# First layer's latent attention: norms applied behind the up-projections, weights scaled by the latent gains, heads staged at other places

## The chip, the cores and the metric

The kernel runs on one core of one Trainium2 chip. The metric is the device time of one execution in microseconds (us), the median of several runs. Its engines work side by side and are tied by semaphores: TensorE (PE in the profile, its queue of weight loads PEld), VectorE (DVE), ScalarE (ACT), GpSimd (POOL) and SyncE (SP), which here issues DMAs.

## What is computed

A trunk of two layers over two sequences of 512 tokens, each with 16 learned tokens in front, model width 1024. The first layer's mixer is multi-head latent attention beside a short gated convolution; the change touches only the attention part. Cut to that:

```python
def rms_norm(x, g):
    y = x * rsqrt(mean(x * x, axis=-1) + 1e-6)
    return y * g

z = h @ w_in                                  # h: the normed tokens
c_q, c_kv, k_r, g_b, g_c, u = split(z)        # 384, 256, 64 and three times 512 columns
q  = (rms_norm(c_q,  q_a_g)  @ w_uq ).reshape(tokens, 4, 192)
kv = (rms_norm(c_kv, kv_a_g) @ w_ukv).reshape(tokens, 4, 256)
k_nope, v = kv[..., :128], kv[..., 128:]
k = concat([k_nope, k_r repeated over the heads])
q, k = rms_norm(q, q_g), rms_norm(k, k_g)
q[..., 128:], k[..., 128:] = rotate(...)      # position tables, cos and sin
attn = softmax(q @ k.T * 192 ** -0.5) @ v
```

Everything else (the convolution, the output projections, the second layer's grouped attention, both SwiGLU blocks) stays as it is.

## The kernel before, in words

**Products.** Every float32 product is made of three matmuls of rounded halves: an operand is split into a high part (a ScalarE copy to the rounded type) and a low part (value minus high part, on VectorE or GpSimd). `product` (lines 166 to 170) issues the three, so nearly all matmuls have the lines 168, 169 and 170. Weights come by DMA from SP's queue into three slots of `stage`, ScalarE rounds them (`round_piece`, line 802) and GpSimd makes the low part (`split_piece`, line 806).

**The stages around the change.** Tokens lie in 10 tiles of 128 rows (5 for each sequence). `gates_steps` makes the convolution's columns of the first projection; `latent_steps` makes the latents and the heads; `attention_phase` runs the attention. Each engine has its own instruction list, written by `sync`, `scalar`, `gpsimd`, `tensor` and `vector` of the steps; an engine works its list strictly in order, so a wait holds up all that stands behind it.

1. **Key latents.** TensorE's `latent(0..9)`: 24 matmuls for each tile into bank 6 or 7. ScalarE's `copy_latent` (lines 823 to 828) takes the sum of squares and copies the tile out.
2. **Key ups, beside the query latents.** For each tile TensorE does `turn(i)` (transposes of the normed latent, line 928), `latent(NT + i)` (24 matmuls) and `up(i)` (12 matmuls of 512 columns). VectorE's `latent_rsqrt` finds the latents' inverse norms for half of the tiles at a time, `norm_latent` (line 1009) multiplies a tile by its inverse norm and by the gain row into `tmp`, from which the transposes read; `round_t` (ScalarE, line 835) and `split_t` (VectorE, line 1033) make the two parts of the transposed tile. ScalarE's `copy_up` (lines 844, 848) takes four sums of squares and copies the heads out, VectorE's `copy_values` (line 1024) the values, GpSimd's `scale_heads` (line 892) multiplies the copied keys by the gain row.
3. **Query ups.** For each tile `turn`, then `up(NT + i)` (18 matmuls of 384 columns); `copy_up`, `scale_heads` over 768 columns, and VectorE's `rotate_queries` (lines 693 to 698), which waits for `scale_heads`. `heads_rsqrt` finds the heads' inverse norms from the sums, by a chain of small operations on VectorE (lines 186, 187, 191 to 193), each of which waits for the one before. For the queries of the first sequence it is cut in two parts. Rotations of the last two tiles, and the inverse norms of the second sequence's keys and queries, are done inside the attention loop (`vector_at`, turns 2, 3, 5 and 7).
4. **Start of the attention.** A head is "staged" by GpSimd (`stage_keys`, lines 1611 and 1613; `stage_queries`, 1635 and 1637): head times inverse norm, into `stage`. TensorE then turns it (`prepare`: five items, keys' two chunks, queries' two chunks and a tail; lines 1798, 1787, 1790), ScalarE rounds (line 1712, 1720) and VectorE splits (1885, 1893). `items_after` says after which query up the first head's items come (the first three behind up 8, two behind up 9), `keys_after` and `queries_after` where GpSimd stages them (behind 5 and 6). The second head's items come in the attention's turns 1, 1, 2, 2 and 3.
5. **Attention loop.** 40 turns (8 heads, 5 query tiles): `scores` (with lines 1816, 1817), minimum on VectorE (1908), exponential on ScalarE (1736), reciprocal (1915), normalising on GpSimd (1672, 1676), turned probabilities (1829, 1835), output products. The exponentials' three buffers lie over `tmp`, `gain_rows` and `rope`; `wait_exponentials` keeps them from being written too early.

Line 1656 clears the tails. The position table is loaded twice, once into `rope` and, behind the weights of the query ups, once into `stage`.

## Time and profile before

| what | value |
|---|---|
| three runs | 2436.57, 2439.05, 2437.43 us; median 2437.43 |
| the profiled execution's own time | 2441.74 us |
| its span | 2439.9 us |
| granted TensorE clock, mean over the span | 0.98 of full speed |
| TensorE busy | 2335.1 us, 96% of the span |

The span is what the profile shows from first to last instruction; 1.8 us of the execution's own time lie outside it. The stages named above stand at these places of the span: key latents to 205 us, key ups to 278 us, query ups to 328 us, attention from 333 us. A row of the timeline has the start, the duration, the engine and line, the instruction with what it writes and reads, and in brackets how long the engine had been idle and what ended the wait. The granted clock is a share of full speed: TensorE's clock has two levels, 2.4 GHz (1.00) and 1.2 GHz (0.50), and a window's number is the mean.

### The profile page before, as it was taken

How to read it: one execution, taken by the hardware profiler on the slowest of the kernel's cores; microseconds unless marked ns; L12 is line 12 of the kernel's file. 1: busy time of each engine (PE TensorE's matmuls, PEld its weight loads, DVE VectorE, ACT ScalarE, POOL GpSimd, SP SyncE). 2: the span in 40 equal slices, each digit the busy share in tenths (PEclk: the TensorE clock that was granted, in tenths of full speed). 3: DMA queues.
4: the chain of work that ended last, by engine and by line, in shares of the span. 5: the costliest groups of instructions: out<-in, count | busy, mean ns of one | idle time of the engine just before them, and what ended most of it. 6: DMA issues, size and time to landing. Idle time of an engine off the chain costs nothing. (4 is left out here: it accounts for less than half of the span.)

```text
span 2439.9 us, 37816 instructions
## 1 busy us (share of the span) xinstructions
PE 2335.1 (96%) x14683; PEld 2130.8 (87%) x14683; DVE 1289.7 (53%) x2093; ACT 906.7 (37%) x1927; POOL 1239.4 (51%) x999
## 2 busy tenths in 40 slices
PE   7999969899999999999998998989999999999998
PEld 7999858899899999999997887888878888888886
DVE  5222667627744444444448467863864444444444
ACT  5125535535422222222225346664532222222221
POOL 1342457644655555555542346764465555555551
PEclk9999979999999999999998999999999999999999
DMA  5131100332211111111112100013211111111111
GB/s 205 44 122 43 42 1 1 135 102 84 61 48 53 48 48 48 43 51 48 53 40 74 39 2 1 2 44 95 82 52 52 52 52 53 52 53 52 53 52 74
DMA packets 186631, 137.69 MB, mean 56 GB/s; under 512 B 7260, under 2 KB 176360, under 8 KB 186456
## 3 DMA queue, kind: packets, MB, share of 16 engines
q1 hardware_dynamic: 186336, 135.20, 17.9%
q8 instruction: 119, 1.95, 0.3%
q14 instruction: 56, 0.46, 0.1%
q10 hardware_dynamic: 120, 0.09, 0.0%
HBM read 122.12 MB, written 12.85 MB: 55 GB/s over the span
## 5 line engine op out<-in xcount | busy, mean ns | idle before, releaser
L2251 POOL TENSOR_TENSOR w_lo<-stage,w_hi 128x512 fp32r<-128x512 f32 x384 | 517.2, 1351 | 638.5 <-ACT w_hi L2152 636.3
L2152 ACT ACTIVATE w_hi<-stage 128x512 fp32r<-128x512 f32 x384 | 239.3, 628 | 585.6 <-PE PS L170 583.0
L2460 DVE TENSOR_TENSOR hT<-hT,PS 128x528 f32<-128x528 f32 (+1 forms) x384 | 267.2, 696 | 335.1 <-PE PS L170 333.8
L168 PE MATMUL PS<-x_hi,w_lo 128*128 128x264 f32 (+2 forms) x1152 | 375.1, 326 | 13.2 <-POOL w_lo L2251 6.8
L169 PE MATMUL PS<-x_lo,w_hi 128*128 128x264 f32 (+2 forms) x1152 | 372.7, 323 | 0.0
L170 PE MATMUL PS<-x_hi,w_hi 128*128 128x264 f32 (+2 forms) x1152 | 372.6, 323 | 0.0
L168 PE MATMUL PS<-s_hi,w_lo 128*128 128x264 f32 (+1 forms) x1104 | 353.7, 320 | 3.1 <-DVE s_lo L2414 3.1
L170 PE MATMUL PS<-s_hi,w_hi 128*128 128x264 f32 (+1 forms) x1104 | 354.2, 321 | 0.0
L169 PE MATMUL PS<-s_lo,w_hi 128*128 128x264 f32 (+1 forms) x1104 | 353.1, 320 | 0.0
L168 PE MATMUL PS<-b_hi,w_lo 128*128 128x264 f32 (+1 forms) x864 | 279.6, 324 | 4.3 <-POOL w_lo L2251 4.3
L169 PE MATMUL PS<-b_lo,w_hi 128*128 128x264 f32 (+1 forms) x864 | 279.2, 323 | 0.0
L170 PE MATMUL PS<-b_hi,w_hi 128*128 128x264 f32 (+1 forms) x864 | 277.7, 321 | 0.0
L168 PEld LDWEIGHTS PS<-x_hi,w_lo 128*128 128x128 f32 x1152 | 219.7, 191 | 26.6 <-POOL w_lo L2251 7.2
L169 PEld LDWEIGHTS PS<-x_lo,w_hi 128*128 128x128 f32 x1152 | 219.3, 190 | 13.0
L170 PEld LDWEIGHTS PS<-x_hi,w_hi 128*128 128x128 f32 x1152 | 219.4, 190 | 12.8
L168 PEld LDWEIGHTS PS<-s_hi,w_lo 128*128 128x128 f32 x1104 | 207.7, 188 | 18.6 <-issue 3.7
L169 PEld LDWEIGHTS PS<-s_lo,w_hi 128*128 128x128 f32 x1104 | 207.4, 188 | 16.6
L170 PEld LDWEIGHTS PS<-s_hi,w_hi 128*128 128x128 f32 x1104 | 207.9, 188 | 15.8
L168 PEld LDWEIGHTS PS<-b_hi,w_lo 128*128 128x128 f32 x864 | 163.3, 189 | 21.0 <-POOL w_lo L2251 5.0
L170 PEld LDWEIGHTS PS<-b_hi,w_hi 128*128 128x128 f32 x864 | 163.5, 189 | 12.7
L169 PEld LDWEIGHTS PS<-b_lo,w_hi 128*128 128x128 f32 x864 | 162.9, 189 | 12.1
L168 PE MATMUL PS<-x_lo,w_lo 128*128 128x264 f32 (+1 forms) x480 | 154.5, 322 | 7.1 <-POOL w_lo L2251 7.1
(316 smaller groups left out, 4946.6 us busy)
## 6 DMA issues: line engine op xcount, KB each, us to landing
stage<-in_ffn_w SPq DMA_DIRECT2D x280, 256.0 KB, 2.8
stage<-in_even_w_out SPq DMA_DIRECT2D x32, 256.0 KB, 2.7
stage<-in_odd_w_out SPq DMA_DIRECT2D x32, 256.0 KB, 2.7
stage<-in_mla_w_in SPq DMA_DIRECT2D x12, 512.0 KB, 6.4
stage<-in_gqa_w_qkv SPq DMA_DIRECT2D x12, 512.0 KB, 3.8
h_spill<-hT SPq DMA_DIRECT2D x8, 528.0 KB, 5.1
hT<-h_spill SPq DMA_DIRECT2D x8, 528.0 KB, 6.8
conv_hi<-s_hi SPq DMA_DIRECT2D x4, 528.0 KB, 2.7
```

The costliest lines, as they stand in the source:

```text
L168: T.matmul(out, a_lo, b_hi, start=first, stop=False)
L169: T.matmul(out, a_hi, b_lo, start=False, stop=False)
L170: return T.matmul(out, a_hi, b_hi, start=False, stop=last)
L2152: A.activation(ring(w_hi, n), source(n), ACT.Copy).then_inc(rounded, 1)
L2251: G.tensor_tensor(ring(w_lo, n), source(n), ring(w_hi, n).bitcast(F32), ALU.subtract).then_inc(split, 1)
L2460: V.tensor_tensor(o, o, sums(st.slot), ALU.add).then_inc(drained, 1)
```

## The change

- The latents are no longer normed before they are turned: `turn` reads the copied latents as they are (it waits for `lat_copied`). The inverse norm is applied behind the up-projection, as ScalarE's scale in `copy_up` and as a scalar in `copy_values`. It is found for all ten tiles at once, and `latent_rsqrt(KV)` stands ahead of the first `split_t` on VectorE.
- The latent gains come in as five more columns of `gain_cols` (two more DMAs on ScalarE's queue; SP has two fewer). GpSimd's `scale_piece` multiplies the five pieces of up weights by them in `stage`, ahead of `round_piece`.
- The queries' gain goes into the keys' gain for the first 128 columns (`k_gain`), and into the position tables for the last 64 (`query_tables`, made by `make_tables` on GpSimd, in `rope`). `scale_heads` stays for the keys (`scale_keys`) and is gone for the queries. The second load of the position table is gone.
- The first head's keys are staged behind query up 0, its queries behind up 1 in the list (they wait for five rotations); items behind ups 2, 3, 7, 8, 8. The second head is staged ahead of the attention loop, its items come in turns 0, 0, 1, 2, 2.
- On VectorE the second sequence's key norms move to step `NT + 1`, the last two rotations to behind the last query up and into turn 1, the second sequence's query norms from turn 7 to 5. The first sequence's query norms are one piece.

```diff
-            g_rows = mid[0:44, 4224:4224 + P]
+            g_rows = mid[0:49, 4224:4224 + P]
...
-                for src, n in ((mla_q_a_g, Q_RANK), (mla_kv_a_g, KV_RANK), (mla_q_g, QK), (mla_k_g, QK)):
+                for src in (mla_q_g, mla_k_g):
...
+                for src, row, n in ((mla_q_a_g, 44, 3), (mla_kv_a_g, 47, 2)):
+                    act.dma_start(g_rows[row:row + n, :], src[0].rearrange("(c p) -> c p", p=P)).then_inc(gains_in, 16)
...
-                act.wait_ge(const_in, 16 * 5)
...
-                pe.wait_ge(gains_in, 16 * 5)
-                T.transpose(PS[:, 2, 0:44], g_rows, ident[0:44, 0:44]).then_inc(gains_t, 1)
+                pe.wait_ge(gains_in, 16 * 7)
+                T.transpose(PS[:, 2, 0:49], g_rows, ident[0:49, 0:49]).then_inc(gains_t, 1)
...
+            def scale_piece(pool, n):
+                kind, k = pieces[n]
+                column = 4 * KC + 3 * CONV_CHUNKS + (3 + k if kind == "ukv" else k)
+                raw = stage[:, (n % 3) * UNIT:(n % 3) * UNIT + widths[kind]]
+                pool.wait_ge(loaded[n % 3], 16 * ((gates.units + n) // 3 + 1))
+                G.tensor_tensor(raw, raw, gain_cols[:, column:column + 1].broadcast_to([P, widths[kind]]),
+                                ALU.mult).then_inc(w_scaled, 1)
+
             def round_piece(act, n):
-                act.wait_ge(loaded[n % 3], 16 * ((gates.units + n) // 3 + 1))
+                if n in scaled_pieces:
+                    act.wait_ge(w_scaled, scaled_pieces.index(n) + 1)
+                else:
+                    act.wait_ge(loaded[n % 3], 16 * ((gates.units + n) // 3 + 1))
...
-                sp.wait_ge(split, gates.units + number[("uq", 1)] + 1)
-                sp.dma_start(query_rope, line_rope).then_inc(table_in, 16)
...
                 def copy_up(n):
                     e, i = divmod(n, NT)
+                    r = rn_lat[e][:, i:i + 1]
+                    act.wait_ge(rn_ready, e + 1)
                     act.wait_ge(up_done, n + 1)
...
-                        last = A.activation(heads_to[e][:, i, hd * size:(hd + 1) * size], part, ACT.Square,
+                        last = A.activation(heads_to[e][:, i, hd * size:(hd + 1) * size], part, ACT.Square, scale=r,
...
+                def make_tables():
+                    pool.wait_ge(gates.const_in, 16 * 3)
+                    G.tensor_tensor(k_gain[:, 0:NOPE], k_gain[:, 0:NOPE], q_gain[:, 0:NOPE], ALU.mult).then_inc(tables_made, 1)
+                    shape = [P, TILES, 2, ROPE // 2]
+                    halves = q_gain[:, NOPE:QK].rearrange("p (w f) -> p w f", w=2).unsqueeze(1).broadcast_to(shape)
+                    for c in range(2):
+                        G.tensor_tensor(query_tables[:, :, :, c, :], tables[:, :, c, :].unsqueeze(2).broadcast_to(shape),
+                                        halves, ALU.mult).then_inc(tables_made, 1)
...
                 for n in range(4, 10):
+                    if n in scaled_pieces:
+                        scale_piece(pool, n)
                     split_piece(pool, n)
+                    if n == 4:
+                        make_tables()
+                pool.wait_ge(tables_made, 3)
                 for i in range(NT):
-                    scale_heads(i)
+                    if i in (4, 5, 7):
+                        scale_piece(pool, number[("uq", (4, 5, 7).index(i))])
+                    scale_keys(i)
                     if i in (4, 5, 7):
                         split_piece(pool, number[("uq", (4, 5, 7).index(i))])
+                pool.wait_ge(scaled, NT)
+                pool.wait_ge(lat_done, 2 * NT)
                 for i in range(NT):
-                    scale_heads(NT + i)
                     then(i)
...
                 def turn(n):
-                    pe.wait_ge(normed, n + 1)
+                    pe.wait_ge(lat_copied, n + 1)
...
-                        last = T.transpose(PS[:, t_bank(n), k * P:(k + 1) * P], tmp[:, at:at + P], ident[:, :])
+                        last = T.transpose(PS[:, t_bank(n), k * P:(k + 1) * P], lat[e][:, i, k * P:(k + 1) * P], ident[:, :])
...
             def rotate_queries(dve, link, i):
-                dve.wait_ge(scaled, NT + i + 1)
+                if i == 0:
+                    dve.wait_ge(tables_made, 3)
+                dve.wait_ge(up_copied, NT + i + 1)
...
-                    V.scalar_tensor_tensor(tmp[:, (n % 2) * Q_RANK:(n % 2) * Q_RANK + rank[e]], lat[e][:, i, 0:rank[e]],
-                                           rn_lat[e][:, i:i + 1], lat_gain[e], ALU.mult, ALU.mult).then_inc(normed, 1)
+                def latent_rsqrt(e):
+                    dve.wait_ge(lat_squared, (e + 1) * NT)
+                    link(V.tensor_scalar(v_stat[:, 0:NT], lat_ssq[e], 1.0 / rank[e], EPS, ALU.mult, ALU.add))
+                    rsqrt(link, v_stat[:, 0:NT], rn_lat[e], t_stat[:, 0:NT])
+                    V.engine_nop().then_inc(rn_ready, 1)
...
-                latent_rsqrt(KV, 0)
-                norm_latent(0)
+                latent_rsqrt(KV)
                 for n in range(2 * NT):
-                    if n + 1 < 2 * NT:
-                        norm_latent(n + 1)
                     split_t(n)
                     if n == NT:
-                        latent_rsqrt(Q, 1)
+                        latent_rsqrt(Q)
...
+                    if n == NT + 1:
+                        heads_rsqrt(dve, link, KV, 1)
...
                 then(NT - 1)
+                rotate_queries(dve, link, NT - 2)
...
-                if n in (2, 3):
-                    rotate_queries(dve, link, NT - 4 + n)
+                if n == 1:
+                    rotate_queries(dve, link, NT - 1)
                 if n == 5:
-                    heads_rsqrt(dve, link, KV, 1)
-                if n == 7:
                     heads_rsqrt(dve, link, Q, 1)
...
-            steps.items_after = {8: (0, 3), 9: (3, 5)}
-            steps.clear_after, steps.keys_after, steps.queries_after = 0, 5, 6
+            steps.items_after = {2: (0, 1), 3: (1, 2), 7: (2, 3), 8: (3, 5)}
+            steps.clear_after, steps.keys_after, steps.queries_after = 0, 0, 1
...
-                    elif u == 1 and L0:
-                        items_at.setdefault((1, 1, 2, 2, 3)[m], []).append(what)
...
                     if L0:
-                        stage_keys(1)
+                        stage_heads(1)
...
-                        if n == 0 and L0:
-                            stage_queries(1)
```

## Rows read from the trace of the kernel before

**Rows 1.** The page, part 1: busy time, share of span and instructions by engine.

```profile
PE 2335.1 (96%) x14683; PEld 2130.8 (87%) x14683; DVE 1289.7 (53%) x2093; ACT 906.7 (37%) x1927; POOL 1239.4 (51%) x999
```

**Rows 2.** Windows: length, busy time (and instructions) per engine, granted clock, DMA share, GB/s.

```profile
205.00:277.00 72.00, 72.00 (x385) 66.39 (x384) 29.36 (x81) 35.45 (x131) 21.00 (x14) 1.00 0.06 18
277.84:332.70 54.86, 42.35 (x227) 39.90 (x226) 36.36 (x88) 29.36 (x117) 26.26 (x18) 0.91 0.13 44
332.70:382.50 49.80, 34.96 (x206) 32.89 (x207) 35.95 (x85) 18.38 (x50) 28.66 (x31) 0.73 0.00 1
384.00:415.30 31.30, 29.63 (x245) 27.62 (x244) 23.19 (x54) 20.48 (x57) 24.66 (x30) 1.00 0.01 1
```

**Rows 3.** Windows of 4 us around one stop of TensorE.

```profile
308.00:312.00 4.00, 2.10 (x8) 2.10 (x9) 3.85 (x11) 0.49 (x1) 1.15 (x1) 0.65 0.01 2
312.00:316.00 4.00, 4.00 (x14) 4.00 (x13) 3.74 (x9) 0.00 (x0) 2.87 (x2) 0.50 0.00 0
316.00:320.00 4.00, 4.00 (x26) 3.93 (x26) 1.68 (x6) 2.63 (x11) 1.39 (x2) 1.00 0.00 0
```

**Rows 4.** Timeline of TensorE: start, duration, instruction, idle before and releaser.

```profile
209.74 0.39 PE L168 MATMUL PS<-up_first,t_kv 128*128 128x512 f32 x1
...
285.11 0.49 PE L928 MATMUL PS<-ident,tmp 128*128 128x128 f32 x3
...
288.62 0.49 PE L928 MATMUL PS<-ident,tmp 128*128 128x128 f32 x3
...
309.90 0.47 PE L928 MATMUL PS<-ident,tmp 128*128 128x128 f32 x1 [4.92 <-DVE tmp L1009]
...
332.70 0.34 PE L168 MATMUL PS<-x_hi,x_lo 128*106 128x264 f32 x1 [3.37 <-DVE x_hi L1893]
...
344.49 0.94 PE L1829 MATMUL PS<-ident,tmp 106*128 106x106 f32 x4 [5.53 <-issue]
...
366.24 1.12 PE L1798 MATMUL PS<-ident,stage 128*128 128x128 f32 x4 [4.76 <-DVE x_lo L1885]
```

**Rows 5.** Timeline of VectorE, 303 to 310 us.

```profile
303.29 1.70 DVE L187 TENSOR_SCALAR rn_all<-stat 128x20 int32<-128x20 int32 x1
...
307.47 1.73 DVE L193 SCALAR_TENSOR_TENSOR rn_all<-stat,rn_all 128x20 f32<-128x20 f32 x1
```

**Rows 6.** Timeline of GpSimd, 303 to 310 us.

```profile
303.12 1.83 POOL L892 TENSOR_TENSOR wide<-wide,gain_rows 128x768 f32<-128x768 f32 x1 [3.19 <-ACT wide L848]
304.91 1.27 POOL L1611 TENSOR_TENSOR stage<-hT,rn_all 128x640 f32<-128x640 f32 x1
...
307.35 1.81 POOL L892 TENSOR_TENSOR wide<-wide,gain_rows 128x768 f32<-128x768 f32 x1
```

**Rows 7.** Timeline of GpSimd, 197 to 209 us.

```profile
197.24 1.85 POOL L806 TENSOR_TENSOR s_lo<-stage,s_hi 128x768 fp32r<-128x768 f32 x1 [8.72 <-ACT s_hi L802]
...
206.53 2.41 POOL L806 TENSOR_TENSOR s_lo<-stage,s_hi 128x1024 fp32r<-128x1024 f32 x1
```

**Rows 8.** Timeline of ScalarE, 204 to 207 us.

```profile
204.56 1.04 ACT L802 ACTIVATE s_hi<-stage 128x1024 fp32r<-128x1024 f32 x1
...
206.45 0.53 ACT L828 ACTIVATE hT<-PS,stat 128x320 f32<-128x320 f32 x1
```

**Rows 9.** Timeline of VectorE, start of a chain of 12 small operations.

```profile
215.75 0.16 DVE L1001 TENSOR_SCALAR tmp<-stat 128x5 f32<-128x5 f32 x1
215.95 0.17 DVE L186 TENSOR_SCALAR stat<-tmp 128x5 int32<-128x5 int32 x1
```

**Rows 10.** Groups of instructions, ScalarE, 200 to 450 us, shapes apart.

```profile
L825 ACT ACTIVATE wide<-PS,stat 128x384 f32<-128x384 f32 x10 | 5.8, 582 | 21.7 <-PE PS L170 21.7
...
L835 ACT ACTIVATE x_hi<-PS 128x384 fp32r<-128x384 f32 x10 | 4.9, 488 | 3.6 <-PE PS L928 3.6
```

**Rows 11.** Timeline of ScalarE's queue and of TensorE, the first 9 us.

```profile
2.90 0.60 ACTq L387 DMA_DIRECT2D mid<-in_conv_w  x1
...
8.26 0.33 PE L557 MATMUL PS<-ident,mid 44*128 44x44 f32 x1 [0.93 <-DMA mid<-in_conv_w]
```

More of the change, by code:

```diff
@@ L181, in program, with rsqrt @@
         vec_steps = [0]
[L183 removed]
+        def rsqrt(link, v, y, t, negative=False):
             guess = float(0x5F3759DF - 2 ** 31 * negative)
@@ L676, in gates_steps @@
             steps.drained, steps.stored, steps.spilled, steps.y_split = drained, stored, spilled, y_split
+            steps.const_in, steps.gains_ready = const_in, gains_ready
             return steps
@@ L684, in program, with rope_heads @@
         v_stat, t_stat = tmp[:, 960:1024], stat[:, 68:68 + 64]
-        def rope_heads(dve, link, xs, cos, sin, scratch, heads, axes, half):
+        def rope_heads(dve, link, xs, tables, scratch, heads, axes, half):
             n = heads * axes * half
@@ L691, in rope_heads @@
             shape = [P, heads, axes, half]
-            c, s = cos.unsqueeze(1).broadcast_to(shape), sin.unsqueeze(1).broadcast_to(shape)
-            V.tensor_tensor(t[0], x1, c, ALU.mult)
-            V.tensor_tensor(t[1], x2, s, ALU.mult)
-            V.tensor_tensor(t[2], x2, c, ALU.mult)
-            link(V.tensor_tensor(t[3], x1, s, ALU.mult))
+            cos1, sin1, cos2, sin2 = (m.unsqueeze(1).broadcast_to(shape) for m in tables)
+            V.tensor_tensor(t[0], x1, cos1, ALU.mult)
+            V.tensor_tensor(t[1], x2, sin2, ALU.mult)
+            V.tensor_tensor(t[2], x2, cos2, ALU.mult)
+            link(V.tensor_tensor(t[3], x1, sin1, ALU.mult))
             V.tensor_tensor(x1, t[0], t[1], ALU.subtract)
@@ L711, in latent_steps @@
             loaded, rounded, split = gates.loaded, gates.rounded, gates.split
[L712 to L713 removed]
+            (lat_done, lat_early, lat_squared, lat_copied, rn_ready, turned, t_rounded, t_split, up_done,
+             up_squared, up_copied, v_copied, scaled, roped, keys_rotated, rn_k_ready, rn_q_ready, tables_made, w_scaled) = (
                 sem(f"lat_{x}") for x in (
[L715 to L716 removed]
+                    "done", "early", "squared", "copied", "rn_ready", "turned", "t_rounded", "t_split", "up_done",
+                    "up_squared", "up_copied", "v_copied", "scaled", "roped", "keys_rotated", "rn_k_ready", "rn_q_ready",
+                    "tables_made", "w_scaled"))
             KV, Q = 0, 1
@@ L784, in t_part @@
                 return (t_q if n >= NT else t_kv)[part][n % 2]
+            scaled_pieces = [n for n, (kind, k) in enumerate(pieces) if kind in ("ukv", "uq")]
             def load_piece(sp, n):
@@ L848, in copy_up @@
                     A.activation(heads_to[e][:, i, :].rearrange("p (b h n) -> p b h n", b=2, h=2),
-                                 src[:, :, :, 0, :] if e == KV else src, ACT.Copy).then_inc(up_copied, 1)
+                                 src[:, :, :, 0, :] if e == KV else src, ACT.Copy, scale=r).then_inc(up_copied, 1)
                 gates.scalar(act, round_piece)
@@ L1023, in copy_values @@
                     dve.wait_ge(up_copied, i + 1)
-                    V.tensor_copy(v_tok0[:, i, :].rearrange("p (b h n) -> p b h n", b=2, h=2),
-                                  ups(KV, 2 * (i % 2))[:, :, :, 1, :]).then_inc(v_copied, 1)
+                    V.tensor_scalar(v_tok0[:, i, :].rearrange("p (b h n) -> p b h n", b=2, h=2),
+                                    ups(KV, 2 * (i % 2))[:, :, :, 1, :], rn_lat[KV][:, i:i + 1], None,
+                                    ALU.mult).then_inc(v_copied, 1)
                 def split_t(n):
@@ L1086, in wait_exponentials @@
                 if n == 1:
-                    act.wait_ge(scaled, 2 * NT)
+                    act.wait_ge(keys_rotated, 1)
                 if n == 2:
-                    act.wait_ge(keys_rotated, 1)
+                    act.wait_ge(roped, NT)
             def wait_scores(pe, n):
@@ L1257, in rotate @@
                 table = tables[:, work[n][1] % TILES]
-                rope_heads(dve, link, xs, table[:, 0], table[:, 1], scratch, heads, 2, 32)
+                rope_heads(dve, link, xs, (table[:, 0], table[:, 1]) * 2, scratch, heads, 2, 32)
                 V.engine_nop().then_inc(roped, 1)
```

93 lines of the change are left out of this document (28 added, 65 removed).

## The prediction

> **What bounds the kernel now.** I read the page first: TensorE is busy 96% of the span [rows 1], so a gain must fill the places where it stands, or runs at its lower clock. The windows show where these are [rows 2]: none in the key ups (72.0 us busy of 72.0, clock 1.00); 12.5 us of standing in the 54.86 us from query up 0 to the first scores; 14.8 us in the 49.80 us of the attention's first ten turns, at a mean clock of 0.73. Ten settled turns take 31.30 us at 1.00. The timeline of TensorE names the stops [rows 4]: 4.92 us ahead of the turn for query up 5 (waiting for the normed latent), 3.37 us ahead of the first scores (waiting for the first head's tail), 5.53 and 4.76 us in the loop. What made the first is in VectorE's and GpSimd's rows side by side: a `heads_rsqrt` operation on 20 columns takes 1.70 or 1.73 us and ends when GpSimd's instruction ends (303.12 + 1.83 = 304.95 against 303.29 + 1.70 = 304.99; 307.35 + 1.81 = 309.16 against 307.47 + 1.73 = 309.20) [rows 5, 6]. Where GpSimd is quiet, such a chain steps on every 0.20 us [rows 9]. So a small operation that meets a GpSimd instruction waits for its end. After the stop the clock stays low: 0.65, 0.50, then 1.00 again [rows 3], so from 309.9 to about 316 us at half speed, 3.0 us lost.
>
> **The change, in order of the span.** The sum is made against the profiled execution, 2441.74 us (span 2439.9 and 1.84 around it), 4.3 above the median of 2437.43.
>
> (a) *Start.* Two more DMAs stand on ScalarE's queue, and TensorE's turn of the gains waits for all. That turn already waited 0.93 us for the last of them, issued at 2.90 in 0.60 us [rows 11]; VectorE's first scaling, and all after it, stands behind. Two more issues cost at most 1.2 us; nothing if they land with the others; a gain is excluded, since the turn waits for more. TensorE is the bound soon after, so it isn't recovered. I take **+0.7**. The two DMAs less on SP's queue and the dropped second table load (with its wait, nothing but values' loads behind it) stand beside full engines: 0.
>
> (b) *First key up.* Here the change adds a chain that TensorE sees. GpSimd finishes the low part of the last query piece but one at 199.1 [rows 7] and only then scales the first key piece. No row has this operation; 1024 columns cost 2.41 with two full operands [rows 7], and at the rate of a repeated operand 1024/640 x 1.27 = 2.0 [rows 6]. Nearest is the latter, I take 2.1: 201.2. ScalarE rounds, 1.04 [rows 8]: 202.3. Low part 2.4: 204.7; low part of the fourth query piece 1.85: 206.6; second key piece scaled: 208.7; rounded: 209.7. ScalarE's list has `copy_latent(9)` behind that rounding, so the tenth sum of squares, ready at 206.45 before [rows 8], comes 0.85 after: 210.6. All ten are now wanted before the first `split_t`. The first operation of `latent_rsqrt` meets GpSimd's low part (209.7 to 212.1) and waits for its end as in [rows 5, 6]; 12 operations of 0.20 then end at 214.5 [rows 9], `split_t` adds 0.4: up 0 starts at 214.9 and not at 209.74 [rows 4]. That is a stop of 5.2 us in a stage that had none, long enough by [rows 3, 4] to bring the clock down: 3.0 more. **+8.2**. Ends: 3.7 (the wait for GpSimd left out, 5.2 less 1.5, and the clock kept) to 10.5 (both scalings at 2.41, a slower return of the clock).
>
> The Trainium skill (GPSIMD Engine Reference, 3.1 Elementwise) gives 4497 ns for a `tensor_tensor` of 2048 float32 columns; half of that, 2.25, is an estimate for a scaled key piece, and by it (b) would be 0.3 larger. [Rows 6, 7] stand on either side of it, and no row shows this operation.
>
> The rest of the key ups: `norm_latent` off VectorE, scaled query pieces on GpSimd (busy 21.0 of 72 us), pointer scales on ScalarE (35.5 of 72): all under a full TensorE [rows 2], 0. `make_tables` (three operations under 1.3 us each, by the 640 columns of [rows 6]) falls in GpSimd's free time ahead of 197.24, before which it stood idle 8.72 us [rows 7]: 0.
>
> (c) *Query ups to first scores*, 54.86 us now. TensorE's own pace is 3.51 us for a tile (285.11 to 288.62) [rows 4], ten make 35.1. The first head's five items lie inside: four chunks of about 0.55 (1.12 at half clock [rows 4]) and a tail of 0.3, 2.5. Stalls that I expect: `heads_rsqrt(KV, 1)`, now at step 11, meets GpSimd's `stage_keys(0)`, which is free to start then: 1.1 on up 2. ScalarE's rounding of an item behind ups 2, 3 and 7: its work for a tile is near the pace, 0.3 each. The queries' norms (12 x 0.20) ahead of `split_t(17)`: 1.1. The last items ahead of `split_t(19)`: 0.6. `scale_heads`, which `rotate_queries` waited for, and `norm_latent`, whose lateness was the 4.92 us, are gone. Then the tail is split before up 9 ends, and the scores follow at once. 35.1 + 2.5 + 3.7 = 41.3: **-13.6**. Ends: 37.6 (no stall) to 47 (one of them long enough for the clock). The trace also prices the new scale: 384 columns take 582 ns with a pointer scale and 488 without [rows 10], so `copy_up`'s five activations grow by 0.47 us a tile. ScalarE, busy 29.36 us in this stage now, 2.9 a tile [rows 2], reaches 3.4: still under 3.51.
>
> (d) *First ten turns*, 49.80 us against 31.30 settled. Of the 18.5 us too much, 34.96 - 29.63 = 5.3 are TensorE at the low clock and 13.2 standing (14.84 less 1.67) [rows 2]; the stops of 5.53 and 4.76 us are the most of it [rows 4]. The first came with the second head's transposes, rotation of tile 8 and the first minimum all in turns 1 and 2; the second with the key norms of the second sequence, now gone to step 11. What is late next: VectorE has rotations 7 and 8 ahead of the first minimum, rotation 9 in turn 1, and 12 small operations in turn 5, between GpSimd's stagings. I leave 8.5 of the 18.5: 5.5 standing, 3 clock. **-10**. Ends: -15 to 0.
>
> Sum: 0.7 + 8.2 - 13.6 - 10 = -14.7; the profiled execution would take 2427.0, the median **2422.7**.
>
> **The rivals.**
> - *The gate is cheap*: GpSimd scales before ScalarE needs it, or the clock holds. Then (b) is about 2 and the median 2416.5. For it: VectorE idles there. Against: the lists' order leaves no freedom. 0.12.
> - *The start of the attention is jammed anew*. GpSimd's four staging operations for the second head (4 x 1.27 = 5.1 us [rows 6]) run while VectorE rotates tiles 7 and 8 ahead of the first minimum. By the rows' rule those small operations wait, the first minimum is up to 5 us later and the clock falls: 9 of the 10 of (d) are lost, 2431.7. 0.16.
> - *Sooner in name only*: the first head's queries still wait for five rotations and norms; (c) gives 9 instead of 13.6: 2427.3. 0.08.
> - *Slower*: the clock stays low after the stop at 210 us, through the key ups, where nothing hides it. At the 0.73 of the first turns [rows 2] 72 us become 98.6, 26.6 more in place of 3.0: 2446.3. It decides from a mean clock of about 0.80 down (72/0.80 = 90, 18 us, against the 17.7 gained otherwise). For it: the first ten turns. Against: these had a new stop every few us, while the key ups are full, and after the 4.92 us stop the clock came back in 6 us [rows 3]. 0.05.
>
> The Trainium skill (SBUF — State Buffer, Who interferes with whom) states the blocking of the second rival: an operation with two SBUF inputs and a GpSimd instruction that reads SBUF take the shared port in order of issue, and the second waits for the whole of the first. The trace agrees, by the four ends compared above. By that rule alone the loser may as well be GpSimd.
>
> **The numbers.** A measurement of this kernel tells about 0.2%, 4.9 us, from no change. My forecast has 0.59. Range 2412 to 2433: it takes in the cheap gate, the jam and the bounds of (b) and (c), not the slower case. Faster 0.84, the same 0.10 (the jam together with a dear gate), slower 0.06.
>
> **What would show it.** Right: a stop of about 5 us ahead of the first product of the key ups, near 210 us, then half clock for about 6; query ups at about 3.5 us a tile with no 4.92 us stop; first scores 41 us after query up 0; scores of turn 10 some 40 us after. Wrong: no stop near 210; a stop over 3 us between query up 9 and turn 3; a clock below 0.8 over the key ups.

## The result, and the profile after

| | kernel before | changed kernel |
|---|---|---|
| median | 2437.98 us (2436.57 to 2440.95, 7 runs) | 2431.02 us (2428.90 to 2431.75, 7 runs) |
| the profiled execution | 2441.74, span 2439.9 | 2430.68, span 2428.9 |
| ratio of the times | | 0.9969, 95% interval 0.9959 to 0.9979 |

The change takes 7.0 us off the kernel, 0.3%. The forecast was 2422.7 from 2437.43, a gain of 14.7: the time lies inside the range of 2412 to 2433, the gain is less than half of what was forecast.

The two profiles differ by more than the medians do: their spans by 11.0 us, their own times by 11.1. The profiled execution of before lies 3.8 us above the median of its runs, that of after 0.3 below. Two differences must be explained: 11.1 against the forecast's 14.7, and the 4.1 between 11.1 and 7.0.

The page's part 1, after; it answers to [rows 1]. TensorE is busy 5.1 us less, at the same number of instructions:

```profile
PE 2330.0 (96%) x14683; PEld 2124.9 (87%) x14683; DVE 1265.3 (52%) x2049; ACT 915.3 (38%) x1927; POOL 1229.5 (51%) x997
```

Windows of after, with the columns of [rows 2]: the key ups with the stop ahead of them, query up 0 to the first scores, first scores to the scores of turn 10, and ten settled turns.

```profile
205.00:284.00 79.00, 74.16 (x382) 67.54 (x380) 21.96 (x59) 39.80 (x131) 26.62 (x18) 0.96 0.05 16
284.84:332.94 48.10, 40.77 (x227) 39.22 (x226) 32.10 (x97) 31.51 (x108) 12.46 (x11) 0.93 0.14 50
332.94:372.07 39.13, 28.61 (x207) 26.67 (x206) 27.26 (x69) 20.69 (x59) 22.45 (x26) 0.87 0.00 1
374.00:405.30 31.30, 29.63 (x245) 27.62 (x244) 23.17 (x55) 20.45 (x57) 25.45 (x31) 1.00 0.01 2
```

The settled turns are what they were, 31.30 us. Query ups and start of the attention took 54.86 and 49.80 us [rows 2] and now take 48.10 and 39.13. But query up 0 starts at 284.84 where it started at 277.84. The timeline of TensorE names the stops, in brackets. The first is new. The next four, in the query ups, stand in the stage where [rows 4] had 4.92 us, and the last two, in the loop, where it had 5.53 and 4.76; the 3.37 us ahead of the first scores are gone, though the next scores wait 1.60 us for a copy of ScalarE (at 335.91, not shown):

```profile
214.24 0.79 PE L168 MATMUL PS<-up_first,t_kv 128*128 128x512 f32 x1 [4.84 <-DVE t_kv L1041]
...
295.05 0.69 PE L168 MATMUL PS<-x_hi,x_lo 128*128 128x384 f32 x1 [2.91 <-DVE x_lo L1041]
...
305.86 0.44 PE L168 MATMUL PS<-x_hi,x_lo 128*128 128x384 f32 x1 [1.32 <-DVE x_lo L1041]
...
317.64 0.44 PE L168 MATMUL PS<-x_hi,x_lo 128*128 128x384 f32 x1 [0.59 <-DVE x_lo L1041]
...
328.14 0.44 PE L168 MATMUL PS<-x_hi,x_lo 128*128 128x384 f32 x1 [2.36 <-DVE x_lo L1041]
...
346.42 0.94 PE L1825 MATMUL PS<-ident,gain_rows 106*128 106x106 f32 x4 [2.88 <-DVE s_hi L1881]
...
358.10 1.11 PE L1794 MATMUL PS<-ident,stage 128*128 128x128 f32 x4 [4.40 <-DVE x_lo L1881]
```

**The stop at 214.24** is the gate's chain. Timeline of GpSimd, 198 to 212 us:

```profile
198.54 1.89 POOL L798 TENSOR_TENSOR stage<-stage,gain_cols 128x1024 f32<-128x1024 f32 x1
201.66 2.42 POOL L810 TENSOR_TENSOR up_first<-stage,up_first 128x1024 fp32r<-128x1024 f32 x1 [1.23 <-ACT up_first L806]
204.23 1.84 POOL L810 TENSOR_TENSOR w_lo<-stage,w_hi 128x768 fp32r<-128x768 f32 x1
206.03 1.89 POOL L798 TENSOR_TENSOR stage<-stage,gain_cols 128x1024 f32<-128x1024 f32 x1
209.09 2.35 POOL L810 TENSOR_TENSOR s_lo<-stage,s_hi 128x1024 fp32r<-128x1024 f32 x1 [1.17 <-ACT s_hi L806]
```

ScalarE's rounding waits for the second scaling (3.80 us idle, then 207.95), the last copies of the latents behind it; VectorE's chain starts in the middle of GpSimd's last row and is held by it:

```profile
209.79 1.67 DVE L1014 TENSOR_SCALAR tmp<-stat 128x10 f32<-128x10 f32 x1 [34.40 <-ACT hT L827]
211.50 0.17 DVE L186 TENSOR_SCALAR stat<-tmp 128x10 int32<-128x10 int32 x1
...
213.76 0.42 DVE L1041 TENSOR_TENSOR t_kv<-PS,t_kv 128x256 fp32r<-128x256 f32 x1
```

209.79 + 1.67 = 211.46 against 209.09 + 2.35 = 211.44. Then up 0 takes 5.5 us in place of 2.95, at the lower of the two clock levels (a product of 512 columns every 0.43 us).

**The stop at 295.05** is the one that was forecast at 1.1 us. `heads_rsqrt(KV, 1)` on VectorE, and GpSimd at the same time (timelines, 288 to 295 us):

```profile
288.52 3.46 DVE L1007 TENSOR_SCALAR tmp<-rn_all 128x20 f32<-128x20 f32 x1
292.02 0.18 DVE L186 TENSOR_SCALAR stat<-tmp 128x20 int32<-128x20 int32 x1
...
294.43 0.56 DVE L1041 TENSOR_TENSOR x_lo<-PS,x_hi 128x384 fp32r<-128x384 f32 x1
```

```profile
288.51 0.98 POOL L1654 MEMSET tails<- 96x512 f32 x2
289.46 1.26 POOL L1609 TENSOR_TENSOR stage<-hT,rn_all 128x640 f32<-128x640 f32 x1
290.69 1.26 POOL L1611 TENSOR_TENSOR stage<-hT,rn_all 128x640 f32<-128x640 f32 x1
```

One operation on 20 columns is held for four GpSimd instructions in a row (two clearings of the tails, two stagings of the keys), 288.51 to 291.95, and ends with the last of them, at 291.98. `split_t(12)`, for which up 2 waits, stands behind the whole chain.

**The stop at 305.86**: VectorE stands idle 6.12 us, since the first head's item, whose rounding ScalarE delivers late, is ahead of `split_t(14)` in its list, and the rotation of tile 1 between the two:

```profile
303.11 0.69 DVE L1881 TENSOR_TENSOR x_lo<-PS,x_hi 128x512 fp32r<-128x512 f32 x1 [6.12 <-ACT x_hi L1708]
303.72 0.28 DVE L687 TENSOR_TENSOR wide<-wide,rope 128x128 f32<-128x128 f32 x1
...
305.25 0.56 DVE L1041 TENSOR_TENSOR x_lo<-PS,x_hi 128x384 fp32r<-128x384 f32 x1
```

**The stop at 328.14**: the last operation of a rotation is held by GpSimd's first staging of the second head, which now runs ahead of the loop (VectorE, then GpSimd, 325 to 329 us):

```profile
326.06 1.35 DVE L692 TENSOR_TENSOR wide<-wide 128x128 f32<-128x128 f32 x1
327.52 0.56 DVE L1041 TENSOR_TENSOR x_lo<-PS,x_hi 128x384 fp32r<-128x384 f32 x1
```

```profile
325.86 1.40 POOL L1609 TENSOR_TENSOR stage<-hT,rn_all 128x640 f32<-128x640 f32 x1 [6.21 <-PE PS L1786]
327.23 1.31 POOL L1611 TENSOR_TENSOR stage<-hT,rn_all 128x640 f32<-128x640 f32 x1
```

Here the held operation has two inputs and ends at 327.41, behind the first staging (327.26) and not behind the second (328.54), though that was ready too.

**The stop at 358.10** is the moved norm of the second sequence's queries, turn 5, again beside GpSimd (here its normalising of probabilities, and the values' low part, 354.10 to 355.36); the item's split waits behind the chain:

```profile
352.96 0.91 DVE L1007 TENSOR_SCALAR tmp<-rn_all 128x20 f32<-128x20 f32 x1
353.91 0.27 DVE L186 TENSOR_SCALAR stat<-tmp 128x20 int32<-128x20 int32 x1
354.21 1.18 DVE L187 TENSOR_SCALAR rn_all<-stat 128x20 int32<-128x20 int32 x1
...
357.35 0.69 DVE L1881 TENSOR_TENSOR x_lo<-PS,x_hi 128x512 fp32r<-128x512 f32 x1
```

### The profile page after: what moved, and what is told of

Read it like the earlier page. It is cut to its first block and busy times, and to the rows that moved or that the text cites. A ratio compares the mean times of both kernels' runs of the same rounds, so it can differ in the third digit from the quotient of the medians.

```text
span 2428.9 us, 37774 instructions
## 1 busy us (share of the span) xinstructions
PE 2330.0 (96%) x14683; PEld 2124.9 (87%) x14683; DVE 1265.3 (52%) x2049; ACT 915.3 (38%) x1927; POOL 1229.5 (51%) x997
```

## The experiments

All are edits of the changed kernel, except the kernel before itself. They ran in three groups, each with the kernel before on the same chip (medians 2437.1, 2436.9 and 2437.5 of 10, 15 and 9 runs). The ratio is always to the kernel before, with its 95% interval. "After" stands at 2430.7 to 2431.0. Each interval is about 3 us each way, so that of a difference between two experiments is some 4 us: whatever is smaller rests on the profiles.

**The changed kernel again.**

> The changed kernel once more, as the base for the three runs beside it: ratio to before 0.997 (0.996 to 0.998), a stop of TensorE of 4.8 us ahead of key up 0 and of 2.9 and 2.4 us ahead of query ups 2 and 9. If the ratio moves by more than 0.001, the gain read from two profiles (11.0 us) and that of the medians (7.0 us) differ by noise of the runs.

Measured: 2430.74 us, 0.9972 [0.9960, 0.9983]. The same stops to 0.03 us up to the first scores (4.84, 2.93, 1.33, 0.15, 0.60, 2.36): they belong to the program, not to chance. Two things are not so firm: the stop in turn 6 is 3.59 us here, for 4.40, and query up 0 starts at 285.86, 1.02 us later. Query ups and first ten turns take 48.19 and 38.89 us, for 48.10 and 39.13.

**The kernel before again**, one profile, to see what the 3.8 us are.

> The kernel before, with a second profile. The first profiled execution took 2441.74 us, above all of its timed runs but near their top. If that one was a chance, this one is nearer to the median of 2437 to 2438, and the query ups and first turns (54.9 and 49.8 us then) take a few us less because the low clock ends sooner behind the same stops. If the 4 us lie elsewhere or are what a profile adds, it takes 2441 again.

Measured: 2437.44 us, span 2435.7. Query ups and first ten turns of this second profile:

```profile
277.26:330.74 53.48, 40.95 (x227) 38.50 (x226) 36.38 (x88) 29.35 (x117) 26.29 (x18) 0.94 0.13 45
330.74:378.07 47.33, 33.15 (x207) 31.09 (x207) 34.73 (x85) 18.34 (x50) 28.62 (x30) 0.78 0.00 1
```

Against [rows 2]: 53.48 for 54.86, 47.33 for 49.80, and query up 0 0.58 earlier. Together 4.4 us by turn 10 (378.07 for 382.50), the whole difference of the two executions. The waits for data are the same in the query ups (4.92, 2.71 or 2.72, 3.37); the granted clock is not (0.94 for 0.91, 0.78 for 0.73). TensorE's busy time shows the clock's share: 1.4 us of the 1.4 in the query ups, 1.8 of the 2.5 in the turns. The other 0.7 are stops, among them 3.82 for 5.53 in turn 1 and 5.31 for 4.76 in turn 6.

**The gate taken off up 0.** VectorE's `latent_rsqrt(KV)` behind the first `split_t`, which doesn't need it:

```diff
-                latent_rsqrt(KV)
                 for n in range(2 * NT):
                     split_t(n)
+                    if n == 0:
+                        latent_rsqrt(KV)
```

> The changed kernel, but the latents' key norms are found behind the first split_t and no longer ahead of it. Theory (the stop at key up 0 is the gate of the ten norms and of the rounding behind the scaled piece, and its price is the stop plus the half clock behind it): split_t(0) comes at about 211.0, up 0 starts there and waits once more for the second key piece's low part at 211.4; the stop falls from 4.84 to about 2 us, the clock stays up, 2.8 + 2.7 = 5.5 us less, ratio 0.9947. Rival (the stop costs only its own length, since the clock is low for another reason): 2.8 us less, 0.9957. Second rival (the norms only move the stop to copy_up(0), which wants them): no gain, 0.9969.

Measured: 2423.91 us, 0.9947 [0.9934, 0.9961], 6.8 less than after. TensorE's stop is the rest of the weights' chain:

```profile
211.07 0.50 PE L168 MATMUL PS<-up_first,t_kv 128*128 128x512 f32 x1 [1.71 <-DVE t_kv L1041]
```

Up 0 starts 3.2 us earlier, and takes 3.05 us in place of 5.46: a stop of 1.71 us doesn't cost the clock, the one of 4.84 did. 3.2 + 2.4 = 5.6, and query up 0 starts 5.6 us earlier (279.26): the key ups hide nothing of this stop. Term (b) had both parts right. The rest of the 6.8 is luck in this profile: behind the same stop of 2.36 us, up 9 keeps the high clock (3.41 us, where the changed kernel took 4.96).

**The first scaling sooner as well**, in GpSimd's idle time.

```diff
-                    if n in scaled_pieces:
-                        scale_piece(pool, n)
+                    if n in (6, 8):
+                        scale_piece(pool, n + 1)
```

> The late gate (norms found behind the first split_t), and in addition GpSimd scales each key piece one step sooner: the first ahead of the low part of query piece 2, the second ahead of that of query piece 3. Theory (what is left of the stop, 1.71 us, is the second key piece's low part, late by the chain of scaling, rounding and splitting): its low part ends near 209.0, the stop is gone, 1.7 us less than with the late gate alone: ratio 0.9940. Rival (the low part of query piece 3, now 1.9 us later, stops the tenth latent at its last chunk, or ScalarE's waits only move): 0.9947 or above.

Measured: 2423.69 us, 0.9940 [0.9927, 0.9952]. The stop ahead of up 0 is gone, up 0 starts at 209.66, 1.4 before `gate_late`. The median is 0.2 below that kernel's, the ratio 0.0007 (1.7 us); the intervals decide nothing. In its profile the gain was given back within 80 us, by the clock behind the same stop of up 2. In this run (first block) the lower level lasted through all 18 products (one every 0.32 us, until 294.10), in `qnorm_turn0` below (second block), after the same stop, it never came (0.18 us from the second product on, until 297.67):

```profile
287.98 0.69 PE L168 MATMUL PS<-x_hi,x_lo 128*128 128x384 f32 x1 [2.92 <-DVE x_lo L1041]
288.46 0.52 PE L169 MATMUL PS<-x_lo,x_hi 128*128 128x384 f32 x1
...
293.58 0.52 PE L170 MATMUL PS<-x_hi 128*128 128x384 f32 x1
```

```profile
294.22 0.44 PE L168 MATMUL PS<-x_hi,x_lo 128*128 128x384 f32 x1 [2.93 <-DVE x_lo L1041]
294.50 0.34 PE L169 MATMUL PS<-x_lo,x_hi 128*128 128x384 f32 x1
...
297.33 0.34 PE L170 MATMUL PS<-x_hi 128*128 128x384 f32 x1
```

**GpSimd's staging kept off the key norms.** The stagings wait for both halves of the inverse norms:

```diff
-                    pool.wait_ge(rn_k_ready, 1 + u // HEADS0)
+                    pool.wait_ge(rn_k_ready, 2)
```

> The changed kernel, but GpSimd stages the first head's keys only when the second sequence's key norms are ready. Theory (the 2.9 us stop ahead of query up 2 is one small VectorE operation that lets GpSimd's clearing and two staging instructions pass): that operation falls from 3.46 us to under 1.2 us (the clearing may still hold it), the stop is gone or under 0.5 us, the half clock behind it too: 2.9 + 1.4 = 4 us less, ratio 0.9952. Rival (ScalarE's list sets it: with the pointer scales it is near the pace of TensorE): the operation gets short but the stop only moves to the next tiles, less than 1 us gained.

Measured: 2427.01 us, 0.9958 [0.9945, 0.9970], 3.7 less. The stop of 2.91 us is 0.47, and up 2 takes 3.45 us in place of 4.79; the query ups take 44.34 us for 48.10, so the profile has the 3.7 in the place that was named. VectorE's row, and GpSimd's beside it:

```profile
288.50 1.01 DVE L1007 TENSOR_SCALAR tmp<-rn_all 128x20 f32<-128x20 f32 x1
289.54 0.18 DVE L186 TENSOR_SCALAR stat<-tmp 128x20 int32<-128x20 int32 x1
```

```profile
288.49 0.98 POOL L1654 MEMSET tails<- 96x512 f32 x2
292.06 1.26 POOL L1609 TENSOR_TENSOR stage<-hT,rn_all 128x640 f32<-128x640 f32 x1 [2.58 <-DVEq L1009]
```

So 3.46 us was 1.0 of clearing and 2.5 of staging. That the clearing alone holds it was not in the prediction either.

**The second head's staging kept off the last rotations.** GpSimd waits for seven rotations first:

```diff
+                        first_steps.wait_second(pool)    # pool.wait_ge(roped, 7)
                         stage_heads(1)
```

> The changed kernel, but GpSimd stages the second head only when the rotation of query tile 6 is done. Theory (the 2.36 us stop ahead of query up 9 is split_t(19) queued behind that rotation, which waits for GpSimd's staging): the last operation of rotation 6 falls from 1.35 to 0.28 us, split_t(19) comes about 1.1 us sooner, the stop is 1.3 us and leaves the clock up: 1.1 + 1.5 = 2.6 us less at the first scores; ratio 0.9959. Rival (staging of the second head 1.7 us later pushes rotations 7 and 8 and the first minimum by as much): the gain at up 9 is given back by turn 2, 0.9969.

Measured: 2429.89 us, 0.9966 [0.9954, 0.9979], 0.85 less where 2.6 were expected. The stop of 2.36 us is 1.29 and up 9 takes 3.42 us in place of 4.96, as expected. Two things take most of it back. In this profile the clock behind the untouched stop of up 2 stayed low for longer (6.13 us for 4.79), so the query ups are only 1.25 us shorter. And from the first scores on the kernel takes 0.9 us more: the stop of 2.88 us in turn 1 is 1.44, but the one ahead of it grew from 0.80 to 2.26, that in turn 6 from 4.40 to 5.21. That is the rival, in part. The place is shown, its price alone is not resolved.

**The old staging back.** Only the orders of items and stagings go back to the old ones; norms, scaling and tables stay changed:

```diff
-            steps.items_after = {2: (0, 1), 3: (1, 2), 7: (2, 3), 8: (3, 5)}
-            steps.clear_after, steps.keys_after, steps.queries_after = 0, 0, 1
+            steps.items_after = {8: (0, 3), 9: (3, 5)}
+            steps.clear_after, steps.keys_after, steps.queries_after = 0, 5, 6
...
+                    elif u == 1 and L0:
+                        items_at.setdefault((1, 1, 2, 2, 3)[m], []).append(what)
...
-                        stage_heads(1)
+                        stage_keys(1)
...
+                        if n == 0 and L0:
+                            stage_queries(1)
```

> The changed kernel with the staging undone: first head's items behind ups 8 and 9, the second head's keys staged ahead of the loop and its queries in turn 0, its items in turns 1, 1, 2, 2, 3. Norms, scales, rotations and the order of VectorE's chains stay as changed. Theory (heads staged sooner are what brings the gain, the rest costs): the three items behind up 8 stop TensorE for some 3 us, the first scores come 4 us after up 9 instead of at once, the first turns take 2 to 5 us more; 9 us more than the changed kernel, ratio 1.001 (0.999 to 1.002). Rival (the query ups without scaling and latent norms on VectorE and GpSimd bring the gain): 2 us more, 0.998.

Measured: 2438.43 us (11 runs), 1.0005 [0.9996, 1.0014]. Without the new places of staging and items the change is worth nothing; they bring the 7 to 8 us. Stops like the old ones are back in this profile: 3.23 us ahead of query up 9 (2.71 before), 3.89 ahead of the first scores, 3.98 and 5.57 in the loop; the 4.92 us is gone, and the new 4.84 us stands in its place in the sum. And the stop of up 2 is unchanged, 2.92 us. VectorE's row is the same as after's:

```profile
288.91 3.47 DVE L1007 TENSOR_SCALAR tmp<-rn_all 128x20 f32<-128x20 f32 x1
```

With `scale_heads` gone for the queries, GpSimd has nothing to wait for between query up 0 and its place "behind 5", so it clears and stages at the same moment as before the edit (clearing at 288.90, stagings at 289.86 and 291.08). The stop of up 2 thus comes from the norms' part of the change, which emptied GpSimd's list and put the chain there; of the new stops only 1.32 and 2.36 us belong to the sooner staging.

**The query norms in turn 0** instead of turn 5:

```diff
+                if n == 0:
+                    heads_rsqrt(dve, link, Q, 1)
...
-                if n == 5:
-                    heads_rsqrt(dve, link, Q, 1)
```

> The changed kernel, but the second sequence's query norms are found in turn 0 of the loop instead of turn 5. Theory (the 4.40 us stop of TensorE in turn 6 is this chain of 12 small operations on VectorE, three of them held by GpSimd's stagings; in turn 0 GpSimd is idle and VectorE waits for the first exponential): the chain takes 2.6 us, some 1.1 us of it ahead of the first reciprocal; the 4.4 us stop goes and the half clock of some 4 us behind it (2 us): 4.4 + 2 - 1.1 = 5 us less, ratio 0.9950. Rival (the stop moves into turns 1 to 3, where VectorE has the second head's splits and the tails): under 2 us less, 0.9963 or above.

Measured: 2425.72 us, 0.9951 [0.9938, 0.9963], about 5 less, as the theory said. The stop of 4.40 us is gone. But its profile has only 2.9 us of the 5 from the first scores on, where the edit works (one stop ahead of turn 1 grew from 0.80 to 1.83); 1.3 are the clock that held behind the stop of up 2, and 0.8 lie ahead of query up 0. In this profile the full 5 is luck.

**Rotation ahead of the item's split** in VectorE's list:

```diff
-                    if n > NT:
-                        then(n - NT - 1)
...
+                    if n > NT:
+                        then(n - NT - 1)
```

(the two lines move from ahead of `rotate_queries` to behind it)

> The changed kernel, but VectorE rotates a query tile ahead of splitting an item of the first head, and no longer behind it. Theory (the stops of 1.3 and 2.4 us ahead of query ups 4 and 9, and 0.2 ahead of up 5, are split_t queued behind item and rotation, while VectorE stood idle before, waiting for the item's rounding): the rotation falls into that idle time, the stops of 1.3 and 0.2 go, that of 2.4 falls to under 1 and leaves the clock up (1.5): 1.5 + 1.4 + 1.5 = 4.4 us less, ratio 0.9953. Rival (ScalarE's rounding of the item ahead of round_t is what is late): 1 us less.

Measured: 2428.67 us, 0.9966 [0.9953, 0.9978], 2 less, where 4.4 were expected. The stops of 1.32, 0.16 and 2.36 us are all gone, but the first scores wait 2.26 us for the tail's split, and the clock behind the stop of up 2 stayed low through all of up 2 (6.09 us for 4.79). The pointer scale is still there, so these stops come from the order in VectorE's list and not from ScalarE having too much to do.

**No pointer scale.** `copy_up` without `scale=r`; this leaves the latents' inverse norm out of the copied keys and queries and their sums (the values keep it):

```diff
-  ACT.Square, scale=r,
+  ACT.Square,
...
-  ACT.Copy, scale=r)
+  ACT.Copy)
```

> The changed kernel with ScalarE's inverse norm left out of the copied heads (keys and queries; the values keep it): it prices the pointer scale, 5 activations for each of 20 tiles. Theory (under a full TensorE it is hidden, in the query ups only 0.1 to 0.6 us of it shows where items follow): 0.47 us less of ScalarE for each tile, at most 1.5 us less in all, ratio 0.9963 to 0.9970. Rival (with the pointer scale ScalarE is the bound of the query ups, which makes the miss of 6.8 us there): 4 us or more less, 0.9953 or below.

Measured: 2426.59 us, 0.9956 [0.9944, 0.9969], 4.1 less where the first theory said at most 1.5. The ratio lies between the two that were named (0.9963 and 0.9953), and its interval takes in both; the size is decided by the timeline of TensorE:

```profile
294.55 0.69 PE L168 MATMUL PS<-x_hi,x_lo 128*128 128x384 f32 x1 [2.49 <-DVE x_lo L1041]
...
304.84 0.44 PE L168 MATMUL PS<-x_hi,x_lo 128*128 128x384 f32 x1 [0.87 <-DVE x_lo L1041]
...
325.16 0.45 PE L168 MATMUL PS<-x_hi,x_lo 128*128 128x384 f32 x1 [0.84 <-DVE x_lo L1041]
```

The stops of ups 2 and 4 are about one tile's pointer price shorter (0.42 and 0.45 us), that of 0.59 us is gone, up 9's is shorter by 1.5, and up 9 keeps the high clock (3.42 us for 4.96). The first scores come 43.6 us after query up 0 in place of 48.1: 3.0 of the 4.5 are standing, 1.6 the clock, and the clock has kept behind up 9's stop without any edit too (`gate_late`). So the size is the rival's, but its reason, that ScalarE is the bound of the query ups, isn't shown: in the changed kernel ScalarE is busy 31.51 of the 48.10 us, 3.03 for a tile (288.39 to 291.42) and 3.52 for one with an item, and waits for TensorE ahead of each (0.41 to 5.01 us). Its 0.47 us counts since it stands in a chain: copy, item's rounding, item's split, rotation, `split_t`.

**All places together.** `gate_late`, `early_scale`, `keys_wait`, `second_wait`, and the clearing of the tails behind the stagings of the keys:

```diff
-            steps.clear_after, steps.keys_after, steps.queries_after = 0, 0, 1
+            steps.clear_after, steps.keys_after, steps.queries_after = 1, 0, 1
```

> Late gate, early scaling, the first head's keys staged and the tails cleared only when the second key norms are ready, the second head staged behind rotation 6. Theory (the stops are separate and add up): 6.8 + 1.7 + 3.7 + 1 to 2.6 + 0.5 = 14 to 15 us less than the changed kernel, 2416.5, ratio 0.9912 to 0.9920. Rival (one stop taken away lengthens the next): over 2420, ratio above 0.993.

Measured: 2418.62 us, 0.9919 [0.9906, 0.9933]. And the same with `qnorm_turn0` and `rotate_first`:

> All of the last combination (late gate, early scaling, keys and second head staged later), and in addition the query norms in turn 0 and rotations ahead of items. Theory (stops add up): 2418.6 less 5 and less 3 to 4, 2410.5, ratio 0.9885 to 0.9895. Rival (VectorE is by then the bound of the first turns, and the gain of one is the loss of the other): over 2414, 0.9903 or above.

Measured: **2409.41 us**, 0.9891 [0.9876, 0.9906], 28 us under the kernel before and 21 under the changed one. The two edits bring 9.2 us together, where they brought 5 and 2 alone. In the profiles it is 8.0, and 6.9 of that lie from the first scores on, where `all_fixed` still had a stop of 5.22 us. Query ups to first scores:

```profile
276.98:317.67 40.69, 37.66 (x228) 36.18 (x226) 30.34 (x94) 33.65 (x117) 12.39 (x11) 1.00 0.17 59
```

40.7 us at a granted clock of 1.00, which is what the forecast gave this stage with the stops that it knew. The scores of turn 10 come at 351.20, 33.5 us later, near the settled 31.30.

## Why the prediction was wrong

By the markers of the two profiles, before and after:

| step | forecast | profiles | what |
|---|---|---|---|
| (a) start | +0.7 | -0.5 | key latents end 205.50 and 204.99 |
| (b) first key up | +8.2 | +7.5 | query up 0 at 277.84 and 284.84, less (a) |
| (c) query ups | -13.6 | -6.8 | 54.86 and 48.10 us |
| (d) first ten turns | -10.0 | -10.7 | 49.80 and 39.13 us |
| rest of the kernel | 0 | -0.6 | |
| sum | -14.7 | -11.1 | the two executions' own times |

**(a)** The wait for the DMAs was as forecast: TensorE's turn of the gains waited 1.23 us, for `mla_kv_a_g`, where it had waited 0.93 [rows 11]. What is left of it by the end of the key latents can't be told: that point stands at 205.50 and 204.92 us in two profiles of the kernel before, at 204.99 and 205.92 in two of the changed one, so executions of one program differ by more than the term. The -0.5 of the table is chance.

**(b)** Right, in mechanism and size: the scaling took 1.89 us (2.1 taken), the stop 4.84 (5.2), the clock 2.5 (3.0); `gate_late` gives back 5.6 of these 7.3, all but the 1.71 us of stop that it leaves.

**(c) is the step that failed.** It forecast 3.7 us of standing and none of lost clock; the profile has 7.3 us of standing (2.91 + 1.32 + 0.16 + 0.59 + 2.36) and 2.9 of clock, 1.4 in up 2 and 1.5 in up 9. The excess of 6.5 is the miss of 6.8. Term by term: *`heads_rsqrt(KV, 1)` against `stage_keys(0)`, 1.1*: the place was right, the size was 2.91 and the clock with it. I counted the wait for one GpSimd instruction, the one in work, which is what [rows 5, 6] show; here three more were queued behind it and all went first (`keys_wait`: 3.7 us). *Items, 0.3 each*: 1.32 and 0.16, since the list on VectorE has a late item and a rotation ahead of the split that TensorE waits for; I had counted ScalarE's delay and not what is queued behind it on VectorE (`rotate_first` removes both). *Query norms, 1.1*: 0.59. *Last items, 0.6*: 2.36, since the second head's staging on GpSimd meets the rotation in the last query ups. I had placed that collision in the loop, as the second rival. *The pointer scale*: the arithmetic was right, 0.42 for 0.33 us at 192 columns and 0.90 for 0.81 at 768; "still under 3.51" was true (3.15 us a tile measured) and no cover, since the split waits for ScalarE's last instruction of the tile and not for its mean; `no_pointer_scale` is worth 4.1, of which 1.6 is clock that may have held by chance.

The Trainium skill (ScalarE: Activation LUTs, What ACT_TABLE_LOAD costs) says that each per-partition pointer operand adds about 93 ns to an ACTIVATE; this trace agrees, 90 ns twice above.

**(d)** Right in size against the profile, 39.13 us for 40; what was late next is the stop of 4.40 us in turn 6, from the norms "in turn 5, between GpSimd's stagings" that it named. Its two parts were not right. The forecast left 5.5 us of standing and 3 of clock; by the same sums the profile has 8.9 of standing (39.13 - 28.61 = 10.5, less 1.67) and a busy time 1.0 below the settled one. The sums were unsound too: the first ten turns hold 206 matmul rows and the settled ten 245 [rows 2], so the busy time above the settled one is not the clock's price. That the total came out is in part luck.

**From the execution to the median.** The sum was carried over as it stood, 4.3 us off both. But before's profiled execution was slow in just the stages that the change rebuilds, as its second profile shows: 1.4 of the 6.8 us of (c) and 2.5 of the 10.7 of (d) are time that the first profile happened to lose, 3.2 of it clock. Against the second profile the change gives 5.4 and 8.2. The two second profiles, `before_again` and `after_again`, are 5.5 us apart (2437.44 and 2431.94), less than the medians: two profiles of one pair are uncertain by several us. The excess went with the stages, and should not have been subtracted a second time. This is the other half of the miss: 14.7 forecast, 11.1 between the profiles, 7.0 between the medians.

**The rivals.** *The gate is cheap*: false, 4.84 us and the clock. *Jammed anew*, with 9 us of (d) lost and 2431.7: the time fits by luck, the place doesn't; (d) kept its gain, and the collision with the second head's staging cost one stop in (c). *Sooner in name only*: the wait is there (GpSimd stands 25.16 us until the first head's queries can be staged, at 317.11), but it isn't what is lost in (c): the first item stands behind up 2, at 299.68, and the stops are the ones above. That (c) gave even less than it said (6.8 and not 9) has other causes. *Slower*: false; the clock stayed low through up 0 and then returned, 0.96 over the stage.

**The port.** The Trainium skill (SBUF — State Buffer, Who interferes with whom) has VectorE and GpSimd share a port pair as an exclusive lock for a whole instruction, taken in order of issue. The trace agrees with the lock, by the ends compared above. Of order of issue it shows otherwise in one place: at 288.52 VectorE's operation was waiting already when GpSimd's second, third and fourth instructions began, and all three went ahead. That isn't the general case. At 326.06 the operation was released between GpSimd's first and second staging. Between 200 and 400 us of the fourteen profiles, 86 VectorE operations with two inputs and 20 or 128 columns took at least 0.3 us longer than with GpSimd quiet, and only one of them was passed by a further GpSimd instruction (`staging_back`, at 340.60, 0.65 us). Of 64 such `TENSOR_SCALAR`s with one input tensor and at most 20 columns, 17 were. The profile of the kernel before, open when the forecast was made, already has one of them (VectorE, then GpSimd):

```profile
359.83 2.18 DVE L993 TENSOR_SCALAR tmp<-rn_all 128x20 f32<-128x20 f32 x1
```

```profile
359.72 1.26 POOL L1637 TENSOR_TENSOR stage<-wide,rn_all 128x640 f32<-128x640 f32 x1
360.94 1.04 POOL L1672 TENSOR_TENSOR gain_rows<-gain_rows,stat 104x512 f32<-104x512 f32 x1
```

It ends at 362.01, behind the second of these (361.98). When an operation is passed and when not isn't shown; no run tried other instructions in that place.

**What stays open.** Behind nearly the same stop ahead of up 2 (2.91 to 2.93 us) that up took 4.79, 6.12 and 3.45 us in three kernels, the first and the last 0.8 us apart in when the stop ended. Up 9 took 4.96 or 3.41 us behind the same 2.36. What sets it wasn't separated. In their profiles it hides part of what `early_scale`, `second_wait` and `rotate_first` save in stops, and adds to what `gate_late` and `qnorm_turn0` save; how often it fell either way in the other runs, whose medians are given, isn't known.

## What to carry to other kernels

A small VectorE operation that meets GpSimd costs at least the rest of the instruction in work, and for a `TENSOR_SCALAR` the bound is GpSimd's whole run of ready instructions (3.46 us here, though most held operations went behind the first); give such chains a place where GpSimd waits for something, or make it wait. On each engine, count what is queued behind a late item, not only how late it is: slack in an engine's mean load is no cover for an operation that stands in a chain. When the profiled execution is off its median, ask in which stage: an excess in a stage that the change rebuilds is not carried along.

## What the runs showed of the hardware

- A VectorE operation on 20 columns took 3.46 us beside four GpSimd instructions in a row, 1.01 us beside two clearings that only write, and 0.18 us with GpSimd quiet (`all_fixed`, at 281.33). A rotation's operation on 128 columns, with two inputs, took 1.35 us behind one of two stagings in a row (at 326.06), and 0.28 with GpSimd quiet.
- GpSimd's multiplication by a repeated column takes 1.89 us at 1024 columns, where the same width with two full operands takes 2.35 to 2.42.
- A stop of 1.71 us left TensorE's clock at its higher level; stops of 4.84 and 4.92 us took it to the lower. Stops of 2.36 us (3.41 us for the up behind it in `gate_late`, 4.96 in the changed kernel) and of about 2.9 us (3.45 to 6.13) did either, and one of 3.23 us left it high (`staging_back`, 3.40). Two executions of the kernel before differed by 4.3 us, 3.2 of it in TensorE's busy time at the same stages.
